# The S5 rotation tables' last doubling in the first phase, and the first four gated blocks moved as VectorE squares and transfers

## The reference, cut to what matters

```python
SEQ, D_MODEL, DEPTH, D_FF = 256, 1024, 2, 2816      # batch 1, all float32
def swiglu(x, w_in, w_out):
    g, u = jnp.split(x @ w_in, 2, axis=-1)
    return (jax.nn.silu(g) * u) @ w_out
for layer in range(2):
    if layer == 1: kb, vb, kmean = shared_kv(h, kv_norm, w_kv)
    h = h + 0.5 * swiglu(rmsnorm(h, ffn1_norm[layer]), ffn1_w_in[layer], ffn1_w_out[layer])
    hn = rmsnorm(h, mix_norm[layer])
    h = h + (s5_mixer(hn, ...) if layer == 0 else moba_attention(hn, ...))
    h = h + 0.5 * swiglu(rmsnorm(h, ffn2_norm[layer]), ffn2_w_in[layer], ffn2_w_out[layer])
return rmsnorm(h, final_norm)
```

## Time and profile before

| | |
|---|---|
| median of 3 runs (lowest to highest) | 956.52 us (956.13 to 956.55) |
| the profiled execution's own time | 957.59 us |
| its span | 955.8 us |
| mean granted TensorE clock | 0.998 |
| TensorE matmul busy | 941.7 us (99%) |
| VectorE, ScalarE, GpSimd busy | 620.9, 501.9, 187.1 us |

### The profile page before, as it was taken

How to read it: one execution, slowest core, us unless ns; L and a number is a source line. 1 busy time by engine, 2 the same in 40 slices (tenths; PEclk the granted TensorE clock), 3 DMA queues, 4 the chain that set the end, 5 groups by cost and what they waited for, 6 DMA issues and landing times.

```text
span 955.8 us, 14881 instructions
## 1 busy us (share of the span) xinstructions
PE 941.7 (99%) x5814; PEld 778.8 (81%) x5814; DVE 620.9 (65%) x779; ACT 501.9 (53%) x711; POOL 187.1 (20%) x235
## 2 busy tenths in 40 slices
PE   9999999899999999999999999999999999999997
PEld 7888888688788888888888888888888888888885
DVE  5665779889766566655565566665567565666554
ACT  6654544468455455544653455444458554554441
POOL 4799999811000000000000000000060000000000
PEclk9999999999999999999999999999999999999999
DMA  9856566520266677777778678777761367777761
GB/s 340 279 177 199 178 188 183 152 94 4 91 190 186 192 235 219 212 196 237 215 182 256 183 213 220 204 219 243 211 186 52 106 193 213 217 220 203 184 218 44
DMA packets 137157, 180.11 MB, mean 188 GB/s; under 512 B 95104, under 2 KB 95104, under 8 KB 137088
## 3 DMA queue, kind: packets, MB, share of 16 engines
q1 hardware_dynamic: 136656, 178.56, 63.2%
q10 hardware_dynamic: 432, 0.61, 0.3%
HBM read 167.33 MB, written 1.05 MB: 176 GB/s over the span
## 4 chain that ended last, share of the span: by engine, by line
PE 78%; POOL 15%; issue 2%; DMA 2%; DVE 1%; ACT 1%; SPq 0%; POOLq 0%; ACTq 0%; DVEq 0%
PE ps L1411 76%; POOL tmp L586 7%; POOL sm L586 3%; DMA raw<-in_in 2%; POOL cp L586 2%; POOL w L586 1%; PE ps L1440 1%; DVE w_lo L1060 1%; PE ps L1556 0%; POOL rots L586 0%; POOL rotc L586 0%; PE ps L1416 0%; ACT w_hi L772 0%; ACT pr L1010 0%; POOL cp L684 0%
## 5 line engine op out<-in xcount | busy, mean ns | idle before, releaser
L1060 DVE TENSOR_TENSOR w_lo<-raw,w_hi 128x1024 fp32r<-128x1024 f32 x311 | 398.6, 1285 | 267.7 <-ACT w_hi L772 265.5
L772 ACT ACTIVATE w_hi<-raw 128x1024 fp32r<-128x1024 f32 x311 | 328.5, 1059 | 314.4 <-PE ps L1411 310.9
L1411 PE MATMUL ps<-w_hi,x_hi 128*128 128x512 f32 x896 | 350.9, 392 | 0.8 <-DVE w_lo L1060 0.7
L1411 PE MATMUL ps<-w_hi,x_lo 128*128 128x512 f32 x896 | 348.8, 389 | 0.0
L1411 PE MATMUL ps<-w_lo,x_hi 128*128 128x512 f32 x896 | 348.7, 389 | 0.0
L1411 PEld LDWEIGHTS ps<-w_hi,x_hi 128*128 128x128 f32 x896 | 168.3, 188 | 37.2 <-DVE w_lo L1060 1.5
L1411 PEld LDWEIGHTS ps<-w_hi,x_lo 128*128 128x128 f32 x896 | 168.2, 188 | 35.1
L1411 PEld LDWEIGHTS ps<-w_lo,x_hi 128*128 128x128 f32 x896 | 168.3, 188 | 34.0
L1411 PE MATMUL ps<-w_hi,hid_hi 128*128 128x512 f32 x352 | 137.8, 391 | 2.6 <-DVE w_lo L1060 2.6
L1411 PE MATMUL ps<-w_lo,hid_hi 128*128 128x512 f32 x352 | 137.0, 389 | 0.0
L1411 PE MATMUL ps<-w_hi,hid_lo 128*128 128x512 f32 x352 | 137.0, 389 | 0.0
(11 more groups left out here) (160 smaller groups left out, 612.1 us busy)
## 6 DMA issues: line engine op xcount, KB each, us to landing
raw<-in_in SPq DMA_DIRECT2D x175, 512.0 KB, 4.5
raw<-in_out SPq DMA_DIRECT2D x88, 512.0 KB, 4.1
raw<-in_glu SPq DMA_DIRECT2D x16, 512.0 KB, 4.1
hid_lo<-prod SPq DMA_DIRECT2D x240, 32.0 KB, 2.7
raw<-in_k SPq DMA_DIRECT2D x8, 512.0 KB, 4.6
raw<-in_v SPq DMA_DIRECT2D x8, 512.0 KB, 4.5
raw<-in_q SPq DMA_DIRECT2D x8, 512.0 KB, 4.3
raw<-in_o SPq DMA_DIRECT2D x8, 512.0 KB, 4.4
```

The source lines that it names most:

```text
L772: act.activation(w_hi[:, gu % WS, :], raw[:, gu % RAW, :], ACT.Copy)\
L1060: dve.tensor_tensor(w_lo[:, gu % WS, :], raw[:, gu % RAW, :], w_hi[:, gu % WS, :].bitcast(F32), ALU.subtract)\
L1411: return pe.matmul(o, w, x, start=start, stop=stop, skip_group_check=True)
```

## The change

Three tables of numbers and the code that follows them. `BATCHES` loses its first entry, so TensorE turns only blocks 4 to 7 and 8 to 10 of phase 0. Blocks 0 to 3 go the way of the later phases, in two pairs (`by_pairs`): four transposes on VectorE, 32 more DMAs of 32 KB on SyncE's queue, and the splits `hid_hi` and `hid_lo` two units or more earlier, with `hid_lo` taking both inputs from SBUF. `TABLE_AT` now counts units from the start: the twelve table instructions stand at units 27 to 34, 41 to 43 and 45, where they stood at 45, 47, 49, 51, 53 and 55 to 61. The waits on `hid_moved` and `hid_turned` follow.

```diff
--- before.py
+++ after.py
@@ -68,12 +68,12 @@
 X_OF = {2: [(2, 1)], 4: [(3, 0), (4, 1)], 8: [(5, 0)], 10: [(6, 0)]}
 FINAL = 12
 BATCH = 4
-BATCHES = (0, 4, 8)
+BATCHES = (4, 8)
 MOVE_BEHIND = 8
 SHEETS = [(4, 0), (5, 0), (5, 1), (8, 0)]
 BY_ROWS = [(2, 0), (2, 1), (2, 2), (2, 3), (4, 2), (4, 3), (8, 2), (8, 3), (10, 0), (10, 1), (10, 2), (10, 3)]
 MOVED = 16 * QS * QS
-TABLE_AT = (1, 3, 5, 7, 9, 11, 12, 13, 14, 15, 16, 17)
+TABLE_AT = (27, 28, 29, 30, 31, 32, 33, 34, 41, 42, 43, 45)
 
 
 class Phase:
@@ -154,12 +154,19 @@
 
 def pair_number(p, b):
 
-    return (p.hid0 // p.blocks - 1) * ((p.blocks + 1) // 2) + b // 2
+    if p.n == 0:
+        return b // 2
+    return BATCHES[0] // 2 + (p.hid0 // p.blocks - 1) * ((p.blocks + 1) // 2) + b // 2
+
+
+def by_pairs(p, b):
+
+    return p.name == "in" and (p.n > 0 or b < BATCHES[0])
 
 
 def high_behind(p, phases, b, j):
 
-    if p.n < 2:
+    if p.n < 2 and (p.n, b) not in ((0, BATCHES[0]), (0, BATCHES[0] + 2)):
         return high_batch(p, phases, b, j)
     if p.name == "in" and b >= 4 and b % 2 == 0 and j < 2:
         return [(p, b - 4 + j)]
@@ -338,7 +345,7 @@
             return prod if k % 2 == 0 else prod2
 
         def prod_of(p, b):
-            if p.n == 0:
+            if not by_pairs(p, b):
                 return pair_of(b % BATCH // 2)[:, b % 2]
             return pair_of(pair_number(p, b))[:, b % 2]
 
@@ -512,7 +519,7 @@
 
             def move_hidden(p, b, q):
                 k, n = pair_number(p, b), pair_end(p, b) + 1 - b
-                sp.wait_ge(hid_squares, p.hid0 - phases[0].blocks + b + n)
+                sp.wait_ge(hid_squares, (p.hid0 - phases[0].blocks + BATCHES[0] if p.n else 0) + b + n)
                 for c in range(QS):
                     sp.dma_start(places(b, n, q, c), pieces(p, b, n, q, c)).then_inc(hid_moved[k % 2], 16)
 
@@ -525,8 +532,7 @@
             sheet_moves = {phases[n].unit0 + (b + 1) * phases[n].upb + MOVE_BEHIND + q: (n, b, q)
                            for n, b in SHEETS for q in range(QS)}
             moves = {p.unit0 + (pair_end(p, b) + 1) * p.upb + MOVE_BEHIND + q: (p, b, q)
-                     for p in phases if p.name == "in" and p.n for b in range(0, p.blocks, 2)
-                     for q in range(QS)}
+                     for p in phases for b in range(0, p.blocks, 2) if by_pairs(p, b) for q in range(QS)}
 
             for c in range(DT // 2):
                 sp.dma_start(xt[:, 2 * c:2 * c + 2, :], io["xt"][:, 2 * c:2 * c + 2, :])\
@@ -796,8 +802,8 @@
                                        ACT.Sigmoid).then_inc(act_ready, 1)
 
             def high_hidden(p, b):
-                if p.n == 0:
-                    act.wait_ge(hid_turned, min(b // BATCH * BATCH + BATCH, p.blocks))
+                if not by_pairs(p, b):
+                    act.wait_ge(hid_turned, min(b // BATCH * BATCH + BATCH, p.blocks) - BATCHES[0])
                     act.activation(halves(hid_hi[:, 2 * b:2 * b + 2, :].rearrange("p f x -> p (f x)")),
                                    turned_block(b), ACT.Copy).then_inc(hid_hi_done, 1)
                     return
@@ -1090,9 +1096,11 @@
                 for q in range(TT):
                     dve.wait_ge(act_ready, p.acts0 + TT * b + q + 1)
                     gb = p.block0 + b
-                    if p.n == 0:
-                        if b >= BATCH:
-                            dve.wait_ge(hid_turned, b - BATCH + 1)
+                    if p.name == "in" and not by_pairs(p, b):
+                        if b < BATCHES[1]:
+                            dve.wait_ge(hid_moved[b % BATCH // 2], MOVED)
+                        else:
+                            dve.wait_ge(hid_turned, b - BATCHES[1] + 1)
                         dve.scalar_tensor_tensor(prod_of(p, b)[:, q, :], ps[:, bank(gb, q), HB:NB],
                                                  rs[:, q:q + 1], act_out[:, q, :],
                                                  ALU.mult, ALU.mult).then_inc(drained, 1)
@@ -1109,13 +1117,13 @@
                                                act_out[:, q, :], ALU.mult))
                         dve.tensor_tensor(h[:, q, cols], h[:, q, cols], prod[:, 0, q, :], ALU.add)\
                            .then_inc(drained, 1)
-                if p.name == "in" and p.n:
+                if by_pairs(p, b):
                     dve.wait_ge(drained, p.drained0 + TT * (b + 1))
                     whole = prod_of(p, b).rearrange("p t x -> p (t x)")
                     dve.transpose(whole, whole).then_inc(hid_squares, 1)
 
             def low_hidden(p, b):
-                if p.n == 0:
+                if not by_pairs(p, b):
                     dve.wait_ge(hid_hi_done, min(b // 2 * 2 + 2, p.blocks))
                     dve.tensor_tensor(halves(hid_lo[:, 2 * b:2 * b + 2, :].rearrange("p f x -> p (f x)")),
                                       turned_block(b),
@@ -1212,8 +1220,8 @@
                             after(*done)
                         for turned_one in low_behind(p, phases, b, j):
                             low_hidden(*turned_one)
-                        if n == 1 and p.upb * b + j in TABLE_AT:
-                            last_turn[TABLE_AT.index(p.upb * b + j)]()
+                        if p.unit0 + p.upb * b + j in TABLE_AT:
+                            last_turn[TABLE_AT.index(p.unit0 + p.upb * b + j)]()
                         if j < p.upb - (LEAD if n == 1 and b else 0) and (n, b, j) not in SPLIT_IN_S5:
                             split(p.unit0 + b * p.upb + j + LEAD)
                         if n == 9 and b == 1 and j == 3:
```

## The result

The change made the kernel slower by a little: 959.23 us (958.15 to 960.92, 6 runs) against 956.40 us (956.13 to 956.71, 6 runs), a ratio of 1.0031, 95% interval [1.0022, 1.0041]. In a later set of runs it was 959.86 against 956.32 us, 1.0041 [1.0025, 1.0056]. The profiled execution has a span of 956.1 us, only 0.3 more than before; it is the fastest of its six, which is why a second profile of the same kernel, the slowest of its own six, is shown beside it.

The account below looks back on a forecast made before the run. POOL's last `cp`, through ScalarE's `c_early` and `w_hi`, was taken to hold TensorE's unit 62. Terms 0 + 1.6 + 0 - 0.6 = +1.0 us on the 956.52 us median gave 957.5 us, range 954.3 to 960.3.

Parts of the forecast that it names:

- rival B: In POOL's chain before `cp` ends, POOL pays for every new VectorE instruction: slower, 961 to 963 us; chance 0.21.
- What bounds the kernel: End of phase 1: unit 62 can't begin before the end of POOL's last `cp` plus 3.2 us.
- The transposes and the tables count 0: Ahead of unit 62: 1.35 us of TensorE transposes and the waits at units 60 and 61 go, gaining 0.
- one long wait of 4 to 7 us: Sign at unit 62: TensorE waits once, behind ScalarE's `c_early` and POOL's last `cp`, with none at units 60 and 61.
- `hid_lo`, +1.6 us: Units 17, 18, 25 and 26: four subtractions with both inputs in SBUF delay POOL by 0.4 us each, +1.6 us.
- The transposes on VectorE, 0: At about 30 to 54 us, inside POOL's chain: four single-SBUF-input transposes cost POOL 0.
- upper bound of 0.56 each: Most that each of four VectorE transposes at about 30 to 54 us could cost POOL, together 2.2 us.
- Three tables beneath the power: Units 28 to 30, about 84 to 91 us: two or three table instructions beside POOL's 5.47 us power cost nothing.
- Behind `cp`, -0.6 us: From `cp` to unit 65: without table instructions among the splits, unit 65 begins near 188.9 instead of 189.50, -0.6 us.
- Rival A: From 140 to 187 us tables cost POOL more than in their new places: faster, 954.0 us; chance 0.13.
- far end, 950.0: At unit 62, were POOL's chain not to bind at all: TensorE gets back 6.5 us, giving 950.0 us.

Follow-up runs that it names:

- the fillers: The changed kernel plus 13 or 24 matmuls that nobody reads, ahead of unit 62: 958.06 us (1.0022) and 958.03 us (1.0016) against the kernel before.
- the blocks alone: Changed kernel with the table instructions back at units 45 to 61, so only blocks 0 to 3 moved: 959.58 us, 1.0041 against the kernel before.
- the tables alone: Kernel before with only the table instructions moved to units 27 to 45, TensorE still turning all of phase 0's blocks: 956.96 us, 1.0013.
- late masks: ScalarE's six `half_c` put behind the weight splits of units 62 to 65: change 955.98 us, kernel before 954.72, kernel with only the tables moved 952.54.
- POOL's new order: Behind `cp`, POOL runs masks, `rs` tile 0, `skip_eye`, `rs` tile 1, `decay`, with ScalarE's `half_c` late: change 954.36 us, only tables moved 953.51.

## Why the prediction was right or wrong

The time, 959.23 us, lies in the range (954.3 to 960.3), but on the side of rival B, which had 0.21. I had forecast +1.0 us and got +2.8.

*What bounds the kernel*: right. `cp` pinned unit 62; taking the masks out of its way made the kernel before 1.8 us faster (956.49 to 954.72, on one chip) and removed the wait at unit 62 in all three versions.

*The transposes and the tables count 0*: this is the step that failed, a term put at nothing. "Both gains lie ahead of unit 62, and both only lengthen the wait for it" is what happened: TensorE was ready at 179.87 us by the timeline (179.64 + 0.23; I had said 179.95). But a longer wait isn't free. Before, TensorE idled 2.6 us there, in pieces of 0.30, 0.43, 1.23 and 0.61 us, and kept its clock. Now it idled 4.55 us or more in one piece, and the clock fell. Whether the sum or the single piece matters, no run separates. The missing term is the half clock: 1.8 us on the median by the fillers, 0.9 and 1.6 us by the two profiles. I had expected "one long wait of 4 to 7 us" in so many words and put no price on it.

*`hid_lo`, +1.6 us*: the price was right, 1.8 measured for four. In the changed kernel POOL's power, behind all four, begins at 85.51 us and before at 83.78, 1.73 us later; with the blocks alone it begins at 85.63. The small POOL instructions beside the `hid_lo` at 77.32 and 79.21 took 0.59 us, where I had said about 0.7. The way of this term into the time was not so plain. In the change `cp` ended 0.4 and 1.4 us later in the two profiles (1.0 in both with fillers), not 1.6, because POOL's chain runs faster when VectorE has nothing to do. ScalarE, blocked on `cp`, gives out no `w_hi`, so the last weight split before it stands at 170.34, not 177.54. GpSimd's timeline in the changed kernel shows both rates:

```profile
152.40 3.92 POOL L592 TENSOR_TENSOR tmp<-cp,sm 128x512 f32<-128x512 f32 x2
...
157.77 3.93 POOL L592 TENSOR_TENSOR tmp<-cp,sm 128x512 f32<-128x512 f32 x2
...
173.93 2.20 POOL L592 TENSOR_TENSOR tmp<-cp,sm 128x512 f32<-128x512 f32 x2
...
177.58 2.20 POOL L592 TENSOR_TENSOR tmp<-cp,sm 128x512 f32<-128x512 f32 x2
```

Three instructions take 5.37 us with weight splits beside them (152.40 to 157.77) and 3.65 without (173.93 to 177.58). POOL was some 5 us behind at the start of `cp` (its last `w` ended at 141.5 instead of 136.6), as the tables now ran ahead of that point, and made up most of it. Two such threes at the fast rate give back 3.4 us; the table instructions gone from this stretch would be the rest, which isn't measured by itself. The wait that I counted as cover for TensorE was cover for POOL too. Once the masks are late and VectorE keeps splitting, `cp` ends at 185.78, and the full 1.8 us appears.

*The transposes on VectorE, 0*: right. Beside all four (from 28.63, 32.45, 42.58 and 53.46 us) POOL's small instructions took their plain 0.26 to 0.33 us. For the one at 42.58 to 43.29:

```profile
42.64 0.32 POOL L592 TENSOR_TENSOR tmp<-rots,sm 128x64 f32<-128x64 f32 x1
42.58 0.71 DVE L1123 STREAM_TRANSPOSE prod<-prod 128x512 f32<-128x512 f32 x1
```

The upper bound of 0.56 each is gone, and with it most of rival B's sum. That the time came out slower by more than 0.2%, as B had it, has another reason; that it lies in my range is luck, since the range reached into B for B's price and not for the clock. The Trainium skill (SBUF — State Buffer, section "Who interferes with whom"), which the prediction cited for the price 0, agrees with these rows.

*Three tables beneath the power*: right. They ran there at 85.98, 87.84 and 90.09 us in 0.68 us each, and the power (85.51 to 90.98) took its 5.47 us. In the second profile the first of them was running when the power began (86.15), and the power took 5.81.

*Behind `cp`, -0.6 us*: right where the clock stayed up: with fillers, phase 1 ended 15.3 us after `cp` instead of 15.8, and with the tables alone too. In the change it was 16.2 and 16.9 us.

*Rival A* fell: with the tables alone `cp` ended 0.5 us later, not earlier. Its far end, 950.0, counts the 1.3 us of VectorE's lateness twice, as the 2.65 (183.95 - 181.3) already holds it; the sum is 5.2 us, not 6.5.

## What to carry to other kernels

Savings ahead of a pinned point don't vanish without effect: they make the wait there longer, and a longer wait can have its own price, since TensorE may come back at half clock (here after 4.11 us and more, and not after 3.41). Look first for what holds the pin (here, instructions that a later stage needs, standing in ScalarE's order before work that is due now) and move that; only then are the savings ahead of it worth making. The best kernel here is not the change but half of it plus that move: the tables' new places with late masks, 0.9957 [0.9945, 0.9969] and 0.9971 [0.9960, 0.9982] in two trials. POOL's new order beside it (953.51 against 954.01) is within the scatter of the runs.

## What the runs showed of the hardware that was not expected

- TensorE idle for 3.41 us kept its clock (1.00); idle for 4.11, 4.55 and 5.65 us it fell to 0.50, for 6.8, 3.4 and 6.8 us. With 3.06 us of small matmuls and then 2.75 us of idling it also fell, for 3.4 us. Each is one profile, so this is no rule on how long a wait may be.
- Runs of one kernel scatter by microseconds: the changed kernel's by 2.8 and 3.1 us, those of before by 0.6 in the first set and by 5.0 (953.67 to 958.65, 21 runs) in the next. Between the two profiles of the changed kernel the spans differ by 3.1 us: 1.07 is the later `cp`, 0.76 goes with the longer half clock, and the other 1.27 lies behind phase 1.
- A VectorE instruction with both inputs in SBUF slows POOL, and POOL slows it: `hid_lo` took up to 1.118 us in place of 0.684, and the same three POOL instructions took 3.65 us with VectorE idle and 5.37 with weight splits beside them.
